# Matmul operand buffers moved to differing byte offsets in SBUF, weight slots split into separate tensors

## The reference

```python
px = split_proj(modulate(x, pre_mix_g[l], mx[0], mx[1]) @ w_in[l])      # 1280 tokens x 1024 -> 3584
ox = hgrn_bidir(...)                                                    # 4 heads, two directions
mix_x = concat([hgrn_readout(ox, ...), conv_branch(...)]) @ w_out[l]    # 1024 -> 1024
x = x + mx[2] * rms_norm(mix_x, post_mix_g[l])
hx = swiglu(modulate(x, pre_ffn_g[l], ...), w_gate, w_up, w_down)       # 1024 -> 2816 -> 1024
x = x + mx[5] * rms_norm(hx, post_ffn_g[l])
```

## Time and profile before

| what | value |
|---|---|
| median of 3 runs | 1563.49 us (1558.09 to 1563.95) |
| profiled execution: span from first to last instruction | 1560.8 us |
| TensorE matmuls busy | 1461.7 us (94%), 6789 instructions |
| weight loads busy | 1147.9 us (74%) |
| VectorE, ScalarE, GpSimd busy | 742.3, 375.4, 356.2 us |
| DMA | 101.93 MB, mean 65 GB/s |
| mean granted TensorE clock | 0.968 |

### The profile page before, as it was taken

How to read it: one execution, slowest core, us unless ns; L and a number is a source line. 1 busy time by engine, 2 the same in 40 slices (tenths; PEclk the granted TensorE clock), 3 DMA queues, 4 the chain that set the end, 5 groups by cost and what they waited for, 6 DMA issues and landing times.

```text
span 1560.8 us, 17854 instructions
## 1 busy us (share of the span) xinstructions
PE 1461.7 (94%) x6789; PEld 1147.9 (74%) x6789; DVE 742.3 (48%) x1026; ACT 375.4 (24%) x561; POOL 356.2 (23%) x151
## 2 busy tenths in 40 slices
PE   7699999999999877986998999999999999999995
PEld 1488888888888723435877888888888888888884
DVE  1802387688688798238552231332313323132237
ACT  2521321322131242235342211111111211112113
POOL 1421111111011074202133321222212221222114
PEclk9799999999999987988999999999999999999998
DMA  9110100100000153403221211111111101111022
GB/s 357 50 41 27 41 28 28 41 27 27 27 27 27 55 201 101 156 14 126 91 81 54 81 41 41 55 54 45 36 54 54 54 28 52 54 54 44 23 109 108
DMA packets 92655, 101.93 MB, mean 65 GB/s; under 512 B 3118, under 2 KB 77091, under 8 KB 92610
## 3 DMA queue, kind: packets, MB, share of 16 engines
q1 hardware_dynamic: 92610, 101.32, 19.8%
HBM read 92.92 MB, written 8.39 MB: 65 GB/s over the span
## 4 chain that ended last, share of the span: by engine, by line
PE 81%; DVE 10%; issue 5%; POOL 2%; ACT 2%; DMA 1%; DVEq 0%; POOLq 0%; SPq 0%; ACTq 0%
PE bank L515 79%; DVE conv_sum L1299 2%; DVE Q L1369 1%; DVE S L1401 1%; POOL xres L1195 1%; DVE xfull L1266 1%; DVE part L1319 1%; DVE K L1361 1%; DVE h2f L1557 1%; DVE catS L1488 0%; DVE cat L1507 0%; DMA mask<-masks 0%; PE bank L742 0%; PE bank L628 0%; POOL h2Tb L1129 0%
## 5 line engine op out<-in xcount | busy, mean ns | idle before, releaser
L515 PE MATMUL bank<-hT,ring 128*128 128x512 f32 (+1 forms) x1632 | 365.6, 381 | 2.1 <-POOL hT L1129 1.6
L515 PEld LDWEIGHTS bank<-hT,ring 128*128 128x128 f32 x1632 | 287.7, 190 | 61.1 <-POOL hT L1129 1.8
L1129 POOL TENSOR_TENSOR ring<-ring_in,ring 128x1024 fp32r<-128x1024 f32 x28 | 69.5, 2482 | 402.6 <-ACT ring L838 402.6
L1602 DVE TENSOR_TENSOR y<-bank,y 128x512 f32<-128x512 f32 x160 | 109.9, 690 | 86.8 <-PE bank L515 86.4
L1129 POOL TENSOR_TENSOR more<-raw,more 128x1024 fp32r<-128x1024 f32 x32 | 76.5, 2406 | 312.6 <-ACT more L1056 170.2
L1580 DVE TENSOR_TENSOR mid<-bank,sgm 128x512 f32<-128x512 f32 x44 | 30.4, 692 | 225.9 <-ACT sgm L1080 225.9
L515 PE MATMUL bank<-slotX,mid 128*128 128x512 f32 x480 | 134.8, 389 | 0.0
L515 PE MATMUL bank<-more,mid 128*128 128x512 f32 x480 | 134.8, 389 | 0.0
L515 PE MATMUL bank<-h2Tb,split 128*128 128x512 f32 x528 | 127.5, 401 | 4.3 <-POOL h2Tb L1129 4.3
L515 PE MATMUL bank<-h2Ta,split 128*128 128x512 f32 x528 | 125.0, 396 | 1.2 <-POOL split L1129 1.2
L515 PEld LDWEIGHTS bank<-h2Tb,split 128*128 128x128 f32 x528 | 100.9, 191 | 29.0 <-issue 4.5
(11 more groups left out here) (169 smaller groups left out, 1645.5 us busy)
## 6 DMA issues: line engine op xcount, KB each, us to landing
mraw<-in_w_mod SPq DMA_DIRECT2D x48, 512.0 KB, 6.6
ring_in<-in_w_in SPq DMA_DIRECT2D x28, 512.0 KB, 3.8
raw<-in_ffn_w_gate SPq DMA_DIRECT2D x22, 512.0 KB, 3.8
raw<-in_ffn_w_up SPq DMA_DIRECT2D x22, 512.0 KB, 3.8
raw<-in_ffn_w_down SPq DMA_DIRECT2D x22, 512.0 KB, 3.3
xst<-in_x SPq DMA_DIRECT2D x8, 512.0 KB, 12.4
raw<-in_w_out SPq DMA_DIRECT2D x8, 512.0 KB, 4.8
x1t<-in_x SPq DMA_DIRECT2D x8, 512.0 KB, 3.3
```

Of the source, the lines that this page charges most:

```text
L515: return pe.matmul(o, l, r, start=start, stop=stop, skip_group_check=True)
L1129: return pool.tensor_tensor(lo, full, hi.bitcast(F32), ALU.subtract)
L1602: ins = dve.tensor_tensor(y[:, t, sl], bank[4 + i % 4][:], y[:, t, sl], ALU.add)
```

## The change

The buffers are aligned to 512 bytes and then given offsets of their own. `ring`, `ring_in`, `split` and `more` become lists of one tensor for each slot, so that each slot can have its offset. Every engine still issues the same instructions in the same order, with the same shapes, waits and semaphore updates; only addresses (and names) differ.

```diff
         RAW = 3
+        def align(to, extra=0):
+            free[0] = (free[0] + to - 1) // to * to + extra
+        def slots(name, places, dt=F32R):
+            return [sb(f"{name}{'abcdef'[i]}", [P, 2, DM], dt, offset=o) for i, o in enumerate(places)]
+        align(512)
+        RAW0 = free[0]
         raw = sb("raw", [P, RAW, DM])
-        split = sb("split", [P, 2, 2, DM], F32R)
-        ring = sb("ring", [P, RAW, 2, DM], F32R, offset=spot["raw"])
-        ring_in = sb("ring_in", [P, RAW, 2, DM], offset=spot["raw"])
+        split = slots("split", [RAW0 + 12288, RAW0 + 20480 + 128])
+        RING = [RAW0 + 64, RAW0 + 8192 + 320, RAW0 + 16384 + 352]
+        ring = slots("ring", RING)
+        ring_in = slots("ringin", RING, F32)
+        free[0] = RAW0 + 28672 + 512
...
+        align(512)
         hT = sb("hT", [P, 2, KT, TOK], F32R)
         A0 = spot["hT"]
+        align(512, 192 + 64 - 192)
+        free[0] += 512
         cat = sb("cat", [P, 8, SEQ])
+        align(512)
         W0 = free[0]
...
-        slotX = sb("slotX", [P, 2, DM], F32R, offset=XT0 + 8192)
+        slotX = sb("slotX", [P, 2, DM], F32R, offset=XT0 + 8192 + 192)
         mid = sb("mid", [P, 2, 2, 2, SEQ], F32R, offset=W0)
-        more = sb("more", [P, 3, 2, DM], F32R, offset=W0 + 32768)
-        mid32 = sb("mid32", [P, 2, BANK], offset=W0 + 57344)
+        more = slots("more", [W0 + 32768 + 256, W0 + 32768 + 8192 + 512 + 32, W0 + 32768 + 16384 + 512 + 96])
+        mid32 = sb("mid32", [P, 2, BANK], offset=W0 + 57344 + 768)
```

More of the change, by code:

```diff
@@ L202, in kernel_program @@
         mraw2 = sb("mraw2", [P, KT, DM], offset=A0)
-        vT = sb("vT", [P, 2, BANK], offset=spot["raw"] + RAW * 2 * DM * 4)
+        vT = sb("vT", [P, 2, BANK], offset=RAW0 + RAW * 2 * DM * 4 + 512)
         part7 = sb("part7", [P, SEQ], offset=A0 + 40960)
@@ L230, in wo_part @@
         def wo_part(q, k):
-            return split[:, k, q] if k < 2 else woA[:, k - 2, q]
+            return split[k][:, q] if k < 2 else woA[:, k - 2, q]
         WO_AT = [2, 3, OUT_AT]
@@ L243, in ffn_part @@
         def ffn_part(q, j):
-            return split[:, j, q] if j < 2 else (more[:, j - 2, q] if j < 5 else slotX[:, q])
+            return split[j][:, q] if j < 2 else (more[j - 2][:, q] if j < 5 else slotX[:, q])
         bank = [es.enter_context(nc.psum_tensor(f"bank{i}", [P, BANK], F32)) for i in range(8)]
@@ L422, in load_tile @@
                     sp.wait_ge(gemm_full, s * NUNIT + (last_unit(mine[-1]) + 1 - NUNIT))
-                sp.dma_start(ring_in[:, SLOT[p], 1, :].rearrange("p (k n) -> p k n", k=KT),
+                sp.dma_start(ring_in[SLOT[p]][:, 1, :].rearrange("p (k n) -> p k n", k=KT),
                              win[:, :, bass.ds(col, P)]).then_inc(raw_in[SLOT[p]], 16)
@@ L584, in w @@
                 def w(k):
-                    return [ring[:, SLOT[p], q, k * P:(k + 1) * P] for q in range(2)]
+                    return [ring[SLOT[p]][:, q, k * P:(k + 1) * P] for q in range(2)]
                 if kind == "vt":
@@ L837, in head_hi @@
                 act.wait_ge(raw_in[SLOT[p]], head_fill(s, p) * 16)
-                act.activation(ring[:, SLOT[p], 0], ring_in[:, SLOT[p], 1], ACT.Copy).then_inc(w_hi, 1)
+                act.activation(ring[SLOT[p]][:, 0], ring_in[SLOT[p]][:, 1], ACT.Copy).then_inc(w_hi, 1)
             mod_rows(0)
@@ L1132, in head_lo @@
                 pool.wait_ge(w_hi, s * NTILE + (p + 1))
-                lo_part(ring[:, SLOT[p], 1], ring_in[:, SLOT[p], 1], ring[:, SLOT[p], 0]).then_inc(w_lo, 1)
+                lo_part(ring[SLOT[p]][:, 1], ring_in[SLOT[p]][:, 1], ring[SLOT[p]][:, 0]).then_inc(w_lo, 1)
             for p in range(2):
```

## The result

The changed kernel takes 1569.74 us (median of 10 runs, 1567.41 to 1571.13), the kernel before, run beside it, 1563.95 us. The ratio is 1.004 with a 95% interval of 1.0028 to 1.0053: about 6 us slower, where 7 us less were forecast.

The account below looks back on a forecast made before the run. The prediction took TensorE's time per matmul as the bound, set by weight and moving-operand addresses. Its terms, -14.4 + 6.6 - 0.5 + 0.7 + 0.75 = -6.9 us, took 1563.5 to 1556.6 us; range 1525 to 1580.

Parts of the forecast that it names:

- What bounds the kernel, and that addresses set the price: TensorE, matmuls busy 94% of the span; 512-column matmuls cost 226.8 ns at address difference 0, 233.3 at 32.
- the price is even in the difference; the simplest pattern ... is one that repeats every 64 bytes: Large matmuls: differences 64 to 448 in steps of 64 cost what 0 costs; 352, 416, 480 what 32 costs.
- ring a and b: 960 matmuls with weights in these two ring slots go from 233.3 to 226.8 ns, -6.2 us.
- split, gate and up: 1056 feed-forward matmuls with weights in split go from 233.3 to 226.8 ns, -6.9 us.
- split, output and last down projection: 192 matmuls using split in these projections go from 233.3 to 226.8 ns, -1.2 us.
- more b and more c: 528 + 480 matmuls with weights in these slots go the other way, 6.5 ns dearer each, +6.6 us.
- slotX: Down projection: slot changes every three matmuls may keep 480 matmuls from settling, 0 to 1.5 us; half taken, +0.75.
- 256 columns: The 288 matmuls of 256 columns, at 121.7 ns, gain between nothing and half of 6.5 ns: -0.5 us.
- settling: After a slot switch the low price is not there at once; 66 settling runs cost 0.7 us.
- Only equal remainders settle: Rival: low price only where both streams start equal modulo 512 (or 256); +10.8 us, 1574 us, chance 0.28.
- some differences are nearly free: Rival: the 3720 matmuls at new differences fall to 213.3 ns, 1500 us; half of the way 1532; chance 0.27.
- everything averages out: Rival: prices scatter around the mean of 230.2 ns or placement does nothing; 1563.5 us within 0.5%, chance 0.15.

Follow-up runs that it names:

- experiment 1: Two kernels against the kernel before: slots as separate tensors at the old addresses, ratio 1.0011; two alignments giving all operands remainder 0, 1549.02 us, ratio 0.9908.

## Why the prediction was wrong

**What bounds the kernel, and that addresses set the price** was right. No wait, transfer or other engine moved by enough to matter (TensorE's longest waits in the loop are 6.8 and 4.6 us, before 6.6 and 4.7), and the remainders alone did it (experiment 1). The Trainium skill (SBUF — State Buffer, Who interferes with whom) gives TensorE two independent read ports and says that it never waits on anyone. By that alone the addresses would set no price; the trace agrees for bfloat16, 215.8 ns at all six differences, and for float32r it shows 226.7 against 233.3 ns. Whether the extra is a conflict of the two reads at all, as the prediction took it, is not shown, so these rows don't decide whether the rule about the ports is wrong.

**The step that failed** is "the price is even in the difference; the simplest pattern ... is one that repeats every 64 bytes". It repeats every 256, and it isn't even (192 costs 229.2, 64 costs 233.3). Two known prices, at 0 and at 32 either way, fit many patterns, and the reason given for the simplest one, that a coarse offset only shifts when the reads meet, is refuted by the same rows: differences of 64, 128 and 320 cost about 6 ns more than 0. The time lies inside the stated 1525 to 1580 us only because that range was made wide enough for the rivals; the likeliest case alone had 1552 to 1560. Term by term, with the mean distances of the changed kernel's whole trace at full clock:

| term | forecast, us | measured, us |
|---|---|---|
| ring a and b | -6.2 | +0.1 |
| ring c | 0.0 | +0.3 |
| split, gate and up | -6.9 | -2.7 |
| split, output and last down projection | -1.2 | -0.4 |
| more a | 0.0 | +0.9 |
| more b and more c | +6.6 | +6.0 |
| slotX | +0.75 | +2.4 |
| 256 columns | -0.5 | -1.1 |
| settling | +0.7 | within the distances above |
| sum | -6.9 | +5.5 |

Each measured term is the count times the mean distance after less the mean before: gate and up with split, for instance, 264 x (229.2 + 227.6 + 233.3 + 232.9) ns = 243.7 us against 1056 x 233.3 = 246.4. The sum is 0.35% of 1564 us and lies within the interval. The term of the slots that leave difference 0 was right, because nearly any difference costs that much; the gains were wrong, because nearly none of the new differences is cheap.

**The rivals.** "Only equal remainders settle", modulo 512 or 256, was right in kind (256 is the period). Its 1574 us is some 4.5 us too high for three reasons: more a with `h2Tb` (256) is cheap too, worth 1.5 us; the 528 matmuls at 448 and 192 lie between the two prices, 2.1 us; and the 256 columns saved 1.1. That some differences are nearly free fell: the lowest of all measured at 512 columns is 226.7. That everything averages out fell by the distances; that the time itself moved by less than 0.5%, as it said, comes from gains and losses that happened to be of this size.

**The settling.** The 0.75 us for the alternation in the down projection became 2.4 for slotX: the price there (231.9 ns) is what its difference of 320 costs less a little, not a low price that fails to settle. The 0.7 us for new settling runs was about right: at differences 0 and 256 the runs of 24 cost 227.5 ns where 48 in a row cost 226.8, which is 0.4 us over 528 matmuls.

**Open.** What in TensorE or the memory makes the extra is not shown. Of the types tried only float32r has it, at full clock (at half clock 426.7 ns, twice 213.3), and it changes with a shift of 4 bytes, has period 256 (tested in steps of 32), needs the matmuls next to each other to agree, depends on the width, and does not go away with a shorter weight load. I have no mechanism that gives all of these.

## What to carry to other kernels

Where a kernel is bound by back-to-back float32r matmuls of 512 columns, give the stationary and the moving operands the same address by 256 bytes: two alignments gave 0.9% here, and offsets chosen to be different lost 0.4%. Before believing a rule from two prices in a trace, measure the whole table by itself; 32 runs of 48 matmuls took 0.4 ms of chip time and would have given the sign: the table gives 233.3 ns for 64 and 320, on which the forecast's gains rested. A "nicer" spread of offsets is not safe, and a table is valid for its type and its width only.

## What was not expected of the hardware

The cheap difference depends on the width: 0 is the best at 512 and 504 columns, 64 is better at 500, 496 and 256 (113.5 against 119.8 ns). An offset of 4 bytes in the weights' address costs 5.6 ns a matmul.

Bfloat16 takes 215.8 ns where float32r takes 226.7 at best, so 5% of a float32r stream's time is an extra that bfloat16 doesn't have. The Trainium skill (TensorE: Matmul & The Clock Gate, Back-to-back issue gap) gives N / 2.4 + 2.5 ns as the gap of a single matmul by itself, 215.8 for 512 columns; here a whole stream of bfloat16 matmuls with their weight loads keeps that distance, and a stream of float32r doesn't. The same section of the Trainium skill has such a stream at about 131 ns for 512 columns; no run here comes near it, and for this case the measured 215.8 ns decides.
